# Two-layer encoder trunk on one core: ends of both FFN layers in halves of 512 tokens, down tiles left in PSUM banks, norm roots in PSUM

## What is computed

```
for layer in (0, 1):
    h = rmsnorm(x, g_attn_pre);  a = attention(h)
    x = x + rmsnorm(a, g_attn_post)
    h = rmsnorm(x, g_ffn_pre)
    u = conv3(h @ w_up) + b          # causal, per channel, width 3; 5632 channels
    gate, val = split(u)
    f = (silu(gate) * val) @ w_down  # 2816 -> 1024
    x = x + rmsnorm(f, g_ffn_post)
rmsnorm(x, g) = x * rsqrt(mean(x * x) + eps) * g
```

## Time and profile before

| | us |
|---|---|
| median of 3 runs | 2574.5 (2571.01 to 2575.01) |
| the profiled execution | 2572.73 |
| its span, first to last instruction | 2570.9 |
| mean granted TensorE clock, share of 2.4 GHz | 0.975 |
| TensorE busy in the span | 2398.3 (93%) |
| DVE / POOL / ACT busy | 1786.0 / 1501.9 / 930.2 |

### The profile page before, as it was taken

The page is one execution under the profiler, slowest core; times in us unless marked ns, Lnnn a source line. Parts: engine busy times, 40 slices in busy tenths (PEclk is TensorE's granted clock), DMA queues, the critical chain, the costliest instruction groups (busy, mean ns, idle before and its releaser), DMA issues.

```text
span 2570.9 us, 31553 instructions
## 1 busy us (share of the span) xinstructions
PE 2398.3 (93%) x11916; PEld 1967.6 (77%) x11916; DVE 1786.0 (69%) x1979; ACT 930.2 (36%) x1617; POOL 1501.9 (58%) x1123
## 2 busy tenths in 40 slices
PE   7899999999999999996899998978999999999993
PEld 5688888778888888872678787857778888888882
DVE  3577773796777777778667767663797777767778
ACT  3344451451222222224356565662452222222222
POOL 2222114547999999975441323204637999999982
PEclk9899999999999999998999999989999999999996
DMA  4112234311111111123121212143311111111113
GB/s 156 54 58 74 83 113 171 133 56 50 49 50 50 59 65 50 50 82 121 44 66 34 74 42 74 42 164 138 133 58 58 50 49 50 50 50 66 58 39 125
DMA packets 51238, 191.99 MB, mean 75 GB/s; under 512 B 5904, under 2 KB 6416, under 8 KB 47376
## 3 DMA queue, kind: packets, MB, share of 16 engines
q1 hardware_dynamic: 39184, 148.92, 17.6%
q10 hardware_dynamic: 11904, 41.05, 4.2%
HBM read 146.43 MB, written 29.36 MB: 68 GB/s over the span
## 4 chain that ended last, share of the span: by engine, by line
PE 77%; DVE 13%; ACT 4%; issue 3%; POOL 2%; DMA 1%; ACTq 0%; SPq 0%; POOLq 0%; DVEq 0%
PE ps L1219 9%; PE ps L1217 9%; PE ps L1218 9%; PE ps L1244 6%; PE ps L1246 6%; PE ps L1245 6%; PE ps L1053 3%; PE ps L1025 3%; PE ps L1026 2%; PE ps L1027 2%; PE ps L1090 2%; PE ps L1070 2%; PE ps L1010 2%; PE ps L1145 1%; PE ps L1012 1%
## 5 line engine op out<-in xcount | busy, mean ns | idle before, releaser
L2091 DVE TENSOR_TENSOR a<-a,ps 128x1024 f32<-128x1024 f32 x336 | 408.7, 1217 | 207.2 <-PE ps L1246 195.2
L763 POOL CAST w_hi<-w_raw 128x1024 fp32r<-128x1024 f32 x78 | 89.2, 1143 | 691.3 <-PE ps L1012 236.4
L1244 PE MATMUL ps<-hid,ring 128*128 128x512 f32 x704 | 277.3, 394 | 18.8 <-DVE a L2091 15.3
L845 POOL TENSOR_TENSOR ring<-w_raw,ring 128x512 fp32r<-128x512 f32 x206 | 268.3, 1303 | 16.5
L1245 PE MATMUL ps<-hid,ring 128*128 128x512 f32 x704 | 275.9, 392 | 0.0
L1246 PE MATMUL ps<-hid,ring 128*128 128x512 f32 x704 | 275.8, 392 | 0.0
L1597 ACT ACTIVATE cy<-cx,cv 128x1024 f32<-128x1024 f32 x76 | 94.7, 1246 | 416.8 <-DVE cx L2062 415.5
L1217 PE MATMUL ps<-h,ring 128*128 128x512 f32 x608 | 236.5, 389 | 0.0
L1218 PE MATMUL ps<-h,ring 128*128 128x512 f32 x608 | 236.5, 389 | 0.0
L1219 PE MATMUL ps<-h,ring 128*128 128x512 f32 x608 | 236.5, 389 | 0.0
L843 POOL CAST ring<-w_raw 128x512 fp32r<-128x512 f32 x206 | 128.0, 621 | 123.1 <-PE ps L1172 53.4
(11 more groups left out here) (274 smaller groups left out, 6772.0 us busy)
## 6 DMA issues: line engine op xcount, KB each, us to landing
w_raw<-in_W SPq DMA_DIRECT2D x166, 512.0 KB, 3.4
raw_d<-in_W SPq DMA_DIRECT2D x44, 512.0 KB, 3.8
h<-o_dram ACTq DMA_DIRECT2D x2, 6144.0 KB, 19.8
x_dram<-x ACTq DMA_DIRECT2D x6, 2048.0 KB, 7.2
x<-x_dram SPq DMA_DIRECT2D x2, 4096.0 KB, 12.2
dsw<-draw SPq DMA_DIRECT2D x64, 128.0 KB, 2.3
o_dram<-most SPq DMA_DIRECT2D x6, 1024.0 KB, 4.8
o_dram<-dost SPq DMA_DIRECT2D x6, 1024.0 KB, 3.9
```

What stands on the lines that cost most here:

```text
L845: pool.tensor_tensor(lo, raw[name], hi.bitcast(F32), ALU.subtract).then_inc(item_ready, 1)
L1244: pe.matmul(out, wh, xh, start=True, stop=False)
L2091: dve.tensor_tensor(a[:, f, :], a[:, f, :], src, ALU.add).then_inc(acc_done, 1)
```

## The change

In both layers:

1. The last four down tiles of unit 20 (f = 4 to 7) are not added to a; they stay in the four pairs of banks. The last unit's downs go by halves of 512 tokens in the order f = 4, 5, 6, 7, 0, 1, 2, 3: the first four accumulate in those banks, the other four reuse them as soon as their half is added. All eight of half 0 come before half 1. Each is three matmuls and one DVE add of 128x512.
2. The last unit's value channels (taps), silu, product, high and low parts go by halves, half 0 first.
3. Squares (ACT, 128x512) go to eight free slots for each half instead of two. POOL adds (0,1), (2,3), (4,5); DVE adds those of the first two pairs, and (6,7); TensorE adds the three rests in one bank by three matmuls with ones. No memset, no chain through ss. The root of half 0 is made while half 1's downs run.
4. That root stays in a PSUM bank (`rstd_bank`), and at the boundary so does the root of the new x (`bank(i)`).

At the end of layer 1 only: a * gain * root of half 0 is put between half 1's adds; x + a is made by POOL (7 half tiles), by TensorE with two matmuls with the identity and an ACT copy (7), and by DVE (2). At the boundary stages A and H keep their shares.

```diff
+LAST = [4, 5, 6, 7, 0, 1, 2, 3]
...
         def down_bank(n, f):
+            if n == HT - 1:
+                return down_bank(n - 1, f if f >= 4 else f + 4)
+            if (n, f) == (HT - 2, KT - 1):
+                return 0
             return 4 + 2 * (f % 2) if n == 0 else 2 + 2 * ((KT * (n - 1) + f) % 3)
...
+        def adder(half, k):
+
+            if (half, k) in ((1, KT - 1), (1, KT - 2)):
+                return "dve"
+            return "act" if k % 2 else "pool"
...
@@ SP @@
-                wait_norm(sp, x_new, X_NO[4], n)
+                sp.wait_ge(y_new[adder(half, k)], adder_count(half, k))
@@ POOL, at the end of ffn @@
+                for half in range(2):
+                    for i in (0, 2, 4):
+                        pool.wait_ge(e_sq, 16 * layer + KT * half + i + 2)
+                        pool.tensor_tensor(last_square(half, i), last_square(half, i), last_square(half, i + 1), ALU.add
+                                           ).then_inc(e_pair, 1)
...
+                    if adder(half, k) == "pool":
+                        pool.wait_ge(a_normed, 48 + n + 1)
+                        pool.tensor_tensor(half_of(x, k, half), half_of(x, k, half), half_of(a, k, half), ALU.add
+                                           ).then_inc(y_new["pool"], 1)
@@ TensorE @@
+                    elif (n, f) == (HT - 2, KT - 1):
+                        wait_read(pe, layer, HT - 1, "P4")
+                        wait_read(pe, layer, HT - 1, "P3")
...
+                def last_down(half, i):
...
+                            pe.wait_ge(item_ready, item_count(layer, n, "d2"))
+                            pe.wait_ge(e_lo, layer + 1)
...
+                            pe.wait_ge(hid_lo, u0 + n + 1)
+                    if i >= 4:
+                        pe.wait_ge(e_acc, 16 * layer + KT * half + i - 3)
...
+                    pe.matmul(out, wh, xh, start=f < 4, stop=False, skip_group_check=True)
...
+                def last_sums(half):
+
+                    pe.wait_ge(e_acc, 16 * layer + KT * half + 5)
+                    pe.wait_ge(e_sum, 4 * layer + 2 * half + 1)
+                    pe.matmul(sum_bank(half), ones[:, :], last_square(half, 0), start=True, stop=False)
+                    pe.wait_ge(e_pair, 6 * layer + 3 * half + 3)
+                    pe.matmul(sum_bank(half), ones[:, :], last_square(half, 4), start=False, stop=False)
+                    pe.wait_ge(e_sum, 4 * layer + 2 * half + 2)
+                    pe.matmul(sum_bank(half), ones[:, :], last_square(half, 6), start=False, stop=True).then_inc(a_stat, 1)
...
+                for half in range(2):
+                    for i in range(KT):
+                        if (half, i) == (1, 4):
+                            last_sums(0)
+                        last_down(half, i)
+                last_sums(1)
...
+                    pe.matmul(final_bank(j), ident[:, :], half_of(x, k, half), start=True, stop=False)
+                    pe.wait_ge(a_normed, 48 + n + 1)
+                    pe.matmul(final_bank(j), ident[:, :], half_of(a, k, half), start=False, stop=True).then_inc(y_sum, 1)
@@ ACT @@
-                        rstd(half_of(rstd_x, 0, i), bank(6 + i), D, 0, x_ln, 2 * n + i + 1, x_rstd)
+                        rstd(bank(i), bank(6 + i), D, 0, x_ln, 2 * n + i + 1, x_rstd)
...
                     tap(n, 0)
+                    if n == HT - 1:
+                        tap_half(1)
                     bank_copy(layer, n, "P4")
...
+                    if n == HT - 1:
+                        tap_half(0)
...
+                for half in range(2):
+                    for i in range(KT):
+                        if (half, i) == (1, 4):
+                            last_rstd(0)
...
+                        act.wait_ge(e_acc, 16 * layer + KT * half + i + 1)
+                        act.activation(last_square(half, i), half_of(a, LAST[i], half), ACT.Square).then_inc(e_sq, 1)
+                last_rstd(1)
...
+                    act.activation(half_of(x, k, half), final_bank(j), ACT.Copy).then_inc(y_new["act"], 1)
@@ DVE @@
-                                                 half_of(rstd_a, 0, half), ALU.mult, ALU.mult).then_inc(a_normed, 1)
+                                                 rstd_bank(half), ALU.mult, ALU.mult).then_inc(a_normed, 1)
...
-                            dve.tensor_tensor(hf_part(i), half_of(x, k, half), half_of(rstd_x, 0, half), ALU.mult
+                            dve.tensor_tensor(hf_part(i), half_of(x, k, half), bank(half), ALU.mult
...
-                dve.memset(ss[:, :, :], 0.0).then_inc(ss_add, 1)
...
+                conv_half(0)
+                product_half(0)
+                conv_half(1)
+                tail_half(0)
+                product_half(1)
+                tail_half(1)
+                for i in range(KT):
+                    last_add(0, i)
+                last_add(1, 0)
+                square_pair(0)
+                square_rest(0)
+                for i in range(1, 4):
+                    last_add(1, i)
+                finals = NORM_TILES[:KT] if layer else []
+                for i in range(4, KT):
+                    last_add(1, i)
+                    if i >= 5:
+                        for t in finals[:1]:
+                            scaled(*t)
+                        finals = finals[1:]
+                square_pair(1)
+                for t in finals[:1]:
+                    scaled(*t)
+                square_rest(1)
+                for t in finals[1:]:
+                    scaled(*t)
...
+            def last_adds():
+
+                for k in range(KT):
+                    scaled(1, k)
...
+                for k in (KT - 2, KT - 1):
...
```

More of the change, by code:

```diff
@@ L91, in tensor_steps @@
             out += new[0:2] + [p7] + new[2:3] + [p3] + new[3:4] + [p4] + new[4:]
-    return out + [("dn", HT - 1, f) for f in range(KT)]
+    return out + [("dn", HT - 1, f) for f in LAST]
 def weight_items():
@@ L1251, in ffn @@
                     if sort == "dn":
-                        down(n, what)
+                        if n < HT - 1:
+                            down(n, what)
                     elif n >= PLAIN:
@@ L1272, in _ @@
             ffn(1)
[L1273 removed]
+            last_adds()
         @block.scalar
@@ L1338, in x_norm @@
                     act.activation(half_of(h, 2 * k, half), hf_part(i), ACT.Copy).then_inc(h_hi, 1)
-            def a_norm(n):
-                for half in range(2):
-                    act.wait_ge(a_stat, 2 * n + half + 1)
-                    rstd(half_of(rstd_a, 0, half), bank(4 + half), D, 0, a_ln, 2 * n + half + 1, a_rstd)
             def latents():
@@ new lines, in ffn @@
+                act.wait_ge(conv_done, conv_count(layer, HT - 1, 0))
+                for half in range(2):
+                    g_ = half_of(cy, 0, half)
+                    act.activation(g_, g_, ACT.Silu).then_inc((e_silu, silu_done)[half], 1)
+                act.wait_ge(dn_done, down_count(layer, HT - 2, KT - 1))
+                for half in range(2):
+                    if half:
+                        act.wait_ge(hid_f, u0 + HT)
+                    else:
+                        act.wait_ge(e_f, layer + 1)
+                    act.activation(hid_part(HT - 1, 0)[:, half * HB:(half + 1) * HB], half_of(cy, 0, half), ACT.Copy
+                                   ).then_inc((e_hi, hid_hi)[half], 1)
@@ L1710, in _ @@
             ffn(1)
-            a_norm(3)
+            last_adds()
         @block.vector
@@ new lines, in last_add @@
+                def last_add(half, i):
+                    f = LAST[i]
+                    if half:
+                        dve.wait_ge(dn_done, down_count(layer, HT - 1, i))
+                    else:
+                        dve.wait_ge(e_down, KT * layer + i + 1)
+                    if (half, i) == (0, 0):
+                        dve.wait_ge(acc_done, acc_count(layer, HT - 2, 3))
+                    dve.tensor_tensor(half_of(a, f, half), half_of(a, f, half), bank(down_bank(HT - 1, f) + half), ALU.add
+                                      ).then_inc(e_acc, 1)
@@ new lines, in square_pair, with square_rest @@
+                def square_pair(half):
+                    dve.wait_ge(e_pair, 6 * layer + 3 * half + 2)
+                    dve.tensor_tensor(last_square(half, 0), last_square(half, 0), last_square(half, 2), ALU.add
+                                      ).then_inc(e_sum, 1)
+                def square_rest(half):
+                    dve.wait_ge(e_sq, 16 * layer + KT * (half + 1))
+                    dve.tensor_tensor(last_square(half, 6), last_square(half, 6), last_square(half, 7), ALU.add
+                                      ).then_inc(e_sum, 1)
```

167 lines of the change are left out of this document (125 added, 42 removed).

## The result

| | us |
|---|---|
| changed kernel, median of 4 runs | 2529.32 (2528.28 to 2532.81) |
| kernel before, median of 4 runs beside it | 2574.35 (2571.01 to 2575.01) |
| ratio, with its 95% interval | 0.9833 (0.9818 to 0.9849) |
| span of the profiled execution | 2526.5 (before 2570.9) |

The forecast was 2530.5. Two events mark each end: ACT's last bank copy of up product P4, and the end of POOL's last low part at the boundary, or the last instruction in layer 1. In the tables a time "behind the copy" is counted from the copy of its own layer.

A forecast was written before the change was run, and what follows sets the result against it. TensorE makes 77% of the chain, but the change rewrites two latency chains of 65.4 and 92.4 us. Gains 21 + 22.9 = 43.9 off 2572.73 give 2528.8, plus 1.8 for the median: 2530.5, range 2524 to 2537 (chance 0.55).

The forecast's parts named there:

- Start of the last unit: Both layers: half-width chain and no wait for adds bring the last unit's first down to 2512.35 from 2517.87, 5.5 us.
- Adds and squares: Both ends: half 0 added by 2519.2, squares by 2521.7, root at 2525.3; downs end at 2526.4, before 2532.2.
- End of layer 1: TensorE's identity sums end last, at 2546.5; the span ends at 2550 instead of 2570.9, 21 us gained.
- the 1.5 charged for the clock: End of layer 1: 1.5 us added to TensorE's identity calls for those that start at the lower clock.
- Boundary, POOL's queue: Boundary: after pairs, gain and splits of two weight units, POOL's adds start at 1183.5 instead of 1193.02, 9.5 us.
- Stage A: Boundary x + a: POOL's ten adds take 14.5 us instead of 23.25, DVE far ahead, ending at 1198, before 1216.27.
- The rival of collisions: Boundary: POOL and DVE stay slow beside each other; the boundary gives 10 to 12, all 2542; chance 0.14.
- TensorE's sums "fit": Boundary, new x: TensorE's 16 sums at about 1 us each fit beside POOL's adds of stage A.
- Stage H: Boundary, hf and the high and low parts of new x: 20.1 us instead of 24.8, 4.7 less.
- the case of it staying low: Both ends: TensorE's clock holds at 1.2 GHz throughout, 78 us extra, 2608, slower than before; chance 0.03.
- Pairs from POOL: Both ends: POOL's pairs of squares come 4 us late in each half, 8 to 12 us lost, 2541; chance 0.06.
- One sign of being wrong: Anything moving before 1148 or between the two ends would show the prediction wrong.

The follow-up runs named there:

- late roots: Changed kernel with both groups of sums over partitions after all 16 half downs, and half 0's scaled tiles after all adds; 2523.8 us, ratio 0.9801.
- the first combined one: Changed kernel with late roots, 35 unread matmuls, first gain multiply between POOL's pairs, last sum shared 7 POOL, 6 TensorE, 3 DVE; 2524.2 us, ratio 0.9808.
- the kernel with four buffers: Changed kernel with four buffers instead of two for the squares of the boundary's new x; 2523.99 us, ratio 0.9808.

## Why the prediction was right

The forecast case held: 43.9 forecast, 45.0 by the medians, 42.4 by the two ends. The mechanism held in both ends, with one step wrong and some luck. Step by step, by the prediction's own:

- *Start of the last unit.* First down 6.9 behind the copy, forecast 6.8. The half tap was 0.82, forecast 0.75. Most of the 5.5 us is the bank that nobody waits for: at full width the first down still came at 8.3, against 12.4 before.
- *Adds and squares.* The first sums began 15.25 behind the copy (forecast about 15.5), root of half 0 at 19.4 (19.8). Leaving the down tiles was entered only as adds that go; undone, it cost 5.3 us in each end, 10.6 in all, the largest single part measured.
- *End of layer 1.* The last sum of half 1 ended at 28.4 (forecast 27.0) because the clock cost 1.5 in the sums rather than in the identity calls; these came every 0.86 us and not 0.93, so TensorE ended at 40.4 (41), the span at 44.9 (44.5). TensorE did end last. That the 1.5 charged for the clock was 1.5 is luck: with the same code it was nothing in one other execution, and 2.9 and 3.0 in two more.
- *Boundary, POOL's queue.* Gain multiply at 22.1 (21.9), first add 34.8 (34.9), split 12.7 (13).
- *Stage A.* Last add 48.5 (49.4). But "DVE is far ahead anyway" was wrong as a reason: it is ahead because of the bank. With the root in SBUF the ten adds took 22.3 us, not 13.7. The rival of collisions named the true price and had the wrong side: it is what the change avoids.
- *TensorE's sums "fit".* The step that failed. They end 5.7 us behind POOL's last add instead of 1.85, by the low clock at their start and by POOL's pace, 16 tiles in 13.7 us, which is their own 0.86 a tile.
- *Stage H.* Forecast 4.7 us less, 20.1 behind the last add. From the last sum it went from 22.9 to 16.4, 6.5 less, and with the later sums 22.1 behind the add. The sums' lag, left at its old 1.85, was 3.9 too small, and the gain of stage H itself 1.8 too small: half of the error cancelled. With 0.9 from stage A the boundary gave 21.8 where 22.9 was forecast.

DVE paid nothing for bank operands: 0.74 and 0.68 with a bank, 0.75 and 0.69 without. The Trainium skill, "VectorE: DVE Perf Modes", section on the TRN2 errata, charges 120 cycles for a PSUM source against 58 for an SBUF one, by the prediction's estimate 0.065 us more for each instruction. No run here shows such a charge.

On the rivals: the clock fell to its lower level in both ends, over some 16 us of the boundary (0.57 and 0.58 in the stretches above) and in layer 1's last sums (granted 0.64 over the 4.13 us from 2505.75), and rose again each time the engine was kept busy; the case of it staying low did not come near. Pairs from POOL were never late for `last_sums`: it waited for DVE. The rival of collisions is mis-added: its own terms (3 for gain and split, 2 for the adds, 4.7 for stage H) leave 13.2 of the boundary's 22.9, not 10 to 12. One sign of being wrong did appear to the letter: the stretches ahead of layer 0's copy and between the ends moved, by 1.2 and 3.2 us. They do so from kernel to kernel with the same code, as the last section shows.

## What to carry to other kernels

When a latency chain runs beside GpSimd, look at which VectorE operands lie in SBUF: moving one broadcast operand of a repeated step into a bank was worth 5 to 7 us in each of two stages at the boundary here, without any instruction fewer. Don't start a result early on an in-order engine when its only use is behind the other half's: two groups of sums back to back beat the overlapped order by 2.6 to 5.6 us, by what the clock did in the waits of the other. Before an edit that moved nothing is called worth nothing, compare the granted clock of both traces in that stretch. And when one engine of a stage gets faster, write down the pace of every other one beside it, also of those that "fit".

## What was not expected of the hardware

The granted clock decides what a sum costs, and the same wait does not always bring it down. With late roots the three calls ahead of layer 1's last root took 1.10, 1.02 and 1.02 us after 0.26 us of idling. In seven kernels that don't have them TensorE was idle for 3.30 to 3.37 us at that place; the clock in the sums was then granted at 1.00 in two, 0.64 and 0.61 in two, and 0.50 in three. First the kernel with the root of the new x in SBUF, then the one with unread matmuls at the boundary, whose code here is the same:

```profile
2511.97 1.10 PE L1321 MATMUL ps<-last_sq,ones 128*128 128x512 f32 x2 [3.30 <-DVE last_sq L2331]
2512.90 1.02 PE L1323 MATMUL ps<-last_sq,ones 128*128 128x512 f32 x2
```

```profile
2497.83 2.04 PE L1324 MATMUL ps<-last_sq,ones 128*128 128x512 f32 x2 [3.30 <-DVE last_sq L2334]
2499.66 1.92 PE L1326 MATMUL ps<-last_sq,ones 128*128 128x512 f32 x2
2501.37 1.91 PE L1328 MATMUL ps<-last_sq,ones 128*128 128x512 f32 x2
```

The kernel before shows it too. After 2.99 us of idling in layer 1 the next six matmuls ran at a granted clock of 1.00; after 2.98 us at the same place of layer 0 the clock was down from the third matmul on.

The wander of the code that no edit touches goes with the same clock. "Between" took 1256.9 us at a granted clock of 0.99 in the shortest case (TensorE busy 1204.1), 1269.7 at 0.97 in the longest (busy 1215.2), and 1260.1 to 1265.3 at 0.98 in the other eleven. It shows in whole runs as well: the kernel with the full-width chain took 2529.37 us at a mean granted clock of 0.986 and 2542.23 at 0.979, the first combined one 2522.13 at 0.988 and 2529.7 at 0.983. The clock does not account for all of it (the median of the kernel with four buffers stays open), and what makes it fall in one execution and not in the next was not looked into. The wander is as large as most effects of this study, which is why they are read from stretches, and why a stretch in which TensorE waits has to be read with its clock beside it.
